# Delta-rule operands in DRAM: from one row per head to one region per fetch

## What is computed

```python
u    = tmat @ (v * beta);  wk = tmat @ (kb * exp(g))      # tmat: inverse of a unit triangular 64x64
attn = tril(q @ k.T * decay);  q_head = q * exp(g);  k_tail = k * exp(g_last - g)
def step(state, ...):                                     # one chunk after the other
    v_new = u_i - wk_i @ state
    o_i   = q_i @ state + attn_i @ v_new
    state = state * exp(gl_i) + k_i.T @ v_new
```

## Time and profile before

| | |
|---|---|
| median of 3 runs | 3933.44 us (3933.2 to 3941.19) |
| the profiled execution | 3942.79 us |
| its span | 3941.1 us |
| delta_prep | about 2660 to 2823 us of the span |
| rwkv_prep | to about 3207 us |
| scans | from 3207 us to about 3740 us |

### The profile page before, as it was taken

One profiled execution on the slowest core, in us unless ns is written; L12 is line 12 of the kernel. 1 busy time (PEld: TensorE's weight loads), 2 busy tenths in 40 slices (PEclk: granted clock), 3 DMA queues, 4 the chain that ended last, 5 costly groups with the idle time before them and its releaser, 6 DMA issues. The chain is left out here.

```text
span 3941.1 us, 64424 instructions
## 1 busy us (share of the span) xinstructions
PE 3479.2 (88%) x28352; PEld 2795.1 (71%) x28352; DVE 2077.9 (53%) x2261; ACT 665.9 (17%) x1080; POOL 786.8 (20%) x817
## 2 busy tenths in 40 slices
PE   6999999999998989889999999998677746588698
PEld 3777777777787878778888888886466535576586
DVE  2477777753333645545463353328687845233564
ACT  2122222212000001221111010002233301121100
POOL 0111111110000000025004306100276779100000
PEclk8999999999999999999999999998788867788899
DMA  9444444444332444322232223336767799676443
GB/s 401 147 150 150 151 154 148 150 175 158 124 119 109 162 175 162 118 86 83 84 111 89 86 95 119 112 125 215 232 176 189 193 237 193 161 204 206 141 170 107
DMA packets 359079, 607.74 MB, mean 154 GB/s; under 512 B 136440, under 2 KB 244080, under 8 KB 330128
## 3 DMA queue, kind: packets, MB, share of 16 engines
q1 hardware_dynamic: 305488, 472.23, 37.6%
q0 software_dynamic: 21712, 92.42, 7.2%
q10 hardware_dynamic: 31600, 38.99, 2.8%
HBM read 469.17 MB, written 134.39 MB: 153 GB/s over the span
## 5 line engine op out<-in xcount | busy, mean ns | idle before, releaser
L182 PE MATMUL front_ps<-b_hT,p_wb 128*128 128x512 f32 x4224 | 980.6, 392 | 6.8 <-PEq L94 6.8
L182 PEld LDWEIGHTS front_ps<-b_hT,p_wb 128*128 128x128 f32 x4224 | 790.7, 188 | 187.8 <-issue 20.6
L1772 PE MATMUL in_ps<-b_hT,in_wb 128*128 128x512 f32 (+1 forms) x3264 | 750.0, 390 | 13.5 <-DVE in_wb L1759 13.5
L1772 PEld LDWEIGHTS in_ps<-b_hT,in_wb 128*128 128x128 f32 (+1 forms) x3264 | 606.9, 187 | 147.8 <-DVE in_wb L1759 13.6
L1757 DVE CAST in_wb<-in_raw 128x2048 fp32r<-128x2048 f32 (+1 forms) x68 | 82.6, 1215 | 535.8 <-PE in_ps L1772 531.0
L170 DVE CAST p_wb<-p_raw 128x2048 fp32r<-128x2048 f32 x88 | 108.0, 1227 | 431.7 <-PE front_ps L182 420.8
L813 POOL DMA_DIRECT2D front_mwb<-in_w_ada x128 | 101.3, 796 | 795.8 <-PE front_mps L823 790.6
L1772 PEld LDWEIGHTS in_ps<-b_hc,in_wb 128*128 128x128 f32 (+1 forms) x1728 | 211.4, 189 | 3.2
L1772 PE MATMUL in_ps<-b_hc,in_wb 128*128 128x256 f32 (+1 forms) x1728 | 212.6, 283 | 0.0
L172 DVE TENSOR_TENSOR p_wb<-p_raw,p_wb 128x2048 fp32r<-128x2048 f32 x88 | 201.8, 2293 | 3.0
L1211 PE MATMUL mid_ps<-mid_wb,b_hT 128*128 128x512 f32 x768 | 179.5, 395 | 13.8 <-DVE mid_wb L1196 13.8
(11 more groups left out here) (457 smaller groups left out, 4314.4 us busy)
## 6 DMA issues: line engine op xcount, KB each, us to landing
p_raw<-in_w_in_tiles SPq DMA_DIRECT2D x88, 1024.0 KB, 6.0
in_raw<-in_w_in_tiles SPq DMA_DIRECT2D x67, 1024.0 KB, 4.8
front_mwb<-in_w_ada POOLq DMA_DIRECT2D x128, 512.0 KB, 5.0
open_wb<-in_w_ada_groups SPq DMA_DIRECT2D x32, 1024.0 KB, 11.3
g_scr<-gprep_ob SPq DMA_DIRECT2D x8, 3474.0 KB, 11.5
merge_raw<-in_w_branch_units SPq DMA_DIRECT2D x32, 512.0 KB, 4.5
mid_raw<-in_w_o_parts SPq DMA_DIRECT2D x32, 512.0 KB, 3.3
last_raw<-in_w_out_parts SPq DMA_DIRECT2D x32, 512.0 KB, 3.3
```

Source lines behind the costliest of these rows:

```text
L182: last = self.nc.tensor.matmul(self.ps[:, n % 2, :], self.wb[:, n % 2, x, kt, :], self.hT[:, y, kt, :], start=kt == term == 0, stop=kt == ...
L1772: last = self.nc.tensor.matmul(self.ps[0:width, n % 3, first:end], self.wb[:, n % 2, x, kt, 0:width], h[:, y, kt, :], start=kt == term == ...
```

## The change

The delta operands get two DRAM tensors in place of one. g_chan is indexed by chunk, direction, partition, head and column; g_tok by chunk, partition, head and column. So the heads of one partition lie side by side, and what one fetch takes from one partition is contiguous. The store becomes three DMAs per head, and self.stored counts 80 per head where it counted 48. The computation is untouched.

```diff
-            eng.wait_ge(self.stored[u], 48 * GH // 2)
+            eng.wait_ge(self.stored[u], 80 * GH // 2)
...
     def store(self, sp, i):
         u = i % 2
         sp.wait_ge(self.s["k_out"], i + 1)
-        sp.dma_start(self.g_scr[:, i:i + 1].rearrange("c h p x -> p (c h) x"), self.ob[:, u]).then_inc(self.stored[u], 16)
+        chan, tok = self.g_scr
+        for d in range(2):
+            sp.dma_start(chan[:, d, :, i:i + 1].rearrange("c p h x -> p (c h) x"),
+                         self.ob[:, u, :, G_CH * d:G_CH * (d + 1)]).then_inc(self.stored[u], 16)
+        sp.dma_start(tok[:, :, i:i + 1].rearrange("c p h x -> p (c h) x"), self.ob[:, u, :, 2 * G_CH:G_COLS]).then_inc(self.stored[u], 16)
...
             r = slice(64 * d, 64 * d + 64)
-            rows = self.g_scr[STEPS[k][d]].rearrange("h p x -> p h x")
-            sp.dma_start(self.chan[:, u, d], rows[:, :, G_CH * d:G_CH * (d + 1)]).then_inc(self.loaded[u], 16)
-            sp.dma_start(self.tok[r, u], rows[r, :, 2 * G_CH:G_COLS]).then_inc(self.loaded[u], 16)
+            chan, tok = self.g_scr
+            sp.dma_start(self.chan[:, u, d], chan[STEPS[k][d], d]).then_inc(self.loaded[u], 16)
+            sp.dma_start(self.tok[r, u], tok[STEPS[k][d], r]).then_inc(self.loaded[u], 16)
...
-    g_scr = dram("g_scr", (NCH, GH, P, G_COLS))
+    g_scr = (dram("g_chan", (NCH, 2, P, GH, G_CH)), dram("g_tok", (NCH, P, GH, G_TOK)))
```

More of the change, by code:

```diff
@@ L2485, in heads @@
         if i >= 2 and d == 0:
-            dve.wait_ge(self.stored[u], 48 * (i // 2))
+            dve.wait_ge(self.stored[u], 80 * (i // 2))
         dve.wait_ge(self.s["eg_out"], 2 * i + d + 1)
@@ L2525, in exponentials @@
         if i >= 2:
-            act_e.wait_ge(self.stored[u], 48 * (i // 2))
+            act_e.wait_ge(self.stored[u], 80 * (i // 2))
         self.alink(self.nc.scalar.activation(self.em[:, u], self.em[:, u], ACT.Exp))
```

## The result

The changed kernel takes 4009.34 us (median of 4 runs, 4000.93 to 4011.41) against 3936.21 us for the kernel before beside it (4 runs, 3933.2 to 3941.19): a ratio of 1.0172, with an interval of 1.0156 to 1.0188. That is 73 us slower, where I had forecast no change (3935 us, range 3926 to 3944). The profiled execution is one of 4000.93 us with a span of 3999.2 us, 58 us above that of before.

What follows compares the result with a forecast made beforehand. GpSimd's solver chain was taken to bound the scans, its start hanging on rwkv_prep and the end of delta_prep. Stores +2.7 us and fetches -1.0 us summed to +1.7 us, giving 3935 us on the median, range 3926 to 3944.

Steps and rivals of the forecast that it cites:

- The store, per head: delta_prep's store: 10.9 us against 9.05 per head, +1.8 us; bounds +1.2 and +4.8, priced from r_home's 528 B store.
- The loop over heads: delta_prep: products of head i wait for head i-2's store; 18.8 us of cover, so +1.8 fits without slowing the loop.
- the wait that I had named as a sign of error: delta_prep: VectorE waiting for a store inside the loop over heads would show the forecast wrong.
- The end of the stage, +2.7 us: delta_prep's end: last store issued 0.9 us late and 1.8 longer, +2.7 us; bounds +1.5 and +12.7.
- What it shifts: After delta_prep: the delay passes through rwkv_prep to GpSimd's batch and the end, with no slack seen; last write 2 to 4 us later.
- The fetch, -1 us: Scans, steps 9 to 11: channel part faster, 0.3 us a step; token part stays at 183 GB/s; -1 us in all.
- my other bound of -12.3: Scans' fetches: other bound of the three steps' gain, if the token part moved at 387 GB/s.
- The stores are slow: Rival, delta_prep: scattered 516 B writes at 216 GB/s; +12.7 - 1 = +11.7 us, 3945; chance 0.13.
- The token fetch speeds up: Rival, scans: small pieces were what slowed the token fetch; 2.7 - 12.3 = -9.6 us, 3924; chance 0.14.
- GpSimd isn't the bound: Rival, scans: TensorE's 34.4 us of token waits come off; 3901; chance 0.04.
- TensorE waits longer for its instructions: Rival, scans, steps 8 to 10: five stops in matmul runs grow 2 us each, +10 on +1.7, 3945; chance 0.09.
- The rule I had weighed: Stores: pieces from 512 B run at line rate, so store cost +0 and sum near -1 us; r_home's row spoke against it.

Runs made afterwards that it cites:

- e9: e6 with every piece written and fetched one column later, 4 B past a multiple of 64 B; 3978.85 us, ratio 1.0106 to the kernel before.
- e6: The changed kernel with DRAM rows padded to 144 and 336 columns, each piece beginning at a multiple of 64 B; 3944.20 us, ratio 1.0020.
- e8: The changed kernel with DRAM rows of 132 and 324 columns stored whole, both ends at multiples of 16 B; 3942.31 us, ratio 1.0016.
- e11: The changed kernel with full rows of 132 and 324 columns in DRAM and SBUF, one piece per partition and fetch; 3941.88 us, ratio 1.0011.
- e12: e9 with offset 7 columns instead of 1, so pieces begin 28 B past and end at a multiple of 32 B; 3944.32 us, ratio 1.0009.
- e13: The changed kernel with rows of 136 and 328 columns, pieces beginning at multiples of 32 B; 3940.03 us, ratio 1.0012.
- e16: The changed kernel with chunks' blocks moved apart by 16 unused rows each, partitions' distances unchanged; 3965.43 us, ratio 1.0088.
- e5: The kernel before with each head's store cut by chunks into three DMAs, pieces still 2316 B; 3935.56 us, ratio 0.9995.
- e14: The changed kernel, heads side by side, with partitions' blocks 4608 and 10752 B apart, which also moves chunks apart; 3964.94 us, ratio 1.0063.
- e10: Rows of 144 and 336 columns, heads 0 to 7 beginning 0, 16, 32, 4, 0, 8, 48, 12 B past a multiple of 64 B; 3967.63 us.
- e2: The kernel before, one array and one store per head, but heads side by side in DRAM, pieces 18528 B apart; 3939.48 us, ratio 1.0004.

## Why the prediction was wrong

**The store, per head.** This is the step that failed: the price of the store, "+1.8 us per head", with +4.8 as its upper bound. The runs show +9.3 us per head between the first store and the last, and the token store, the last of the three, lands after 22.1 us, where the single store landed after 11.5. I took r_home's 528 B store as the nearest row and called the two "strided in the same way". Their size was near; their ends weren't, nor was the distance between chunks (1,081,344 B there, 1,056,768 B in the change). A piece of 528 B beginning at a multiple of 528 has one end on a multiple of 32 B (528 is 16.5 times 32), and the pieces of 516 B in heads 1 to 6 have none. e9 against e6 shows what the ends cost, and e8, which has r_home's size, ends and distance, is quick. The upper bound was no bound either, because it was drawn from rows of that same store.

**The loop over heads.** I had found that it does not become slower. That was right for the cost I had put in, and e6, e8, e11 and e12, where the stores behave as priced, show no wait of VectorE for a stored buffer in the whole stage. With the real cost a head's stores outlast the 16.9 us that a head takes on VectorE, so the 18.8 us of cover are used up, and the wait that I had named as a sign of error is there with 53.3 us.

**The end of the stage, +2.7 us.** For small pieces as such, with one even end, the stage is 4.5 to 6.1 us longer (e6 to e8 and e11 to e13), and VectorE's idle time at its end grows by as much (21.32 us in e6, 15.77 before). This lies inside the recorded bounds of 1.5 and 12.7, but it is about twice the 2.7. The 516 B pieces of e6 move 276 GB/s where I had taken 302, and head 7's store is issued 2.4 us later than before, counted from head 0's, where I had 0.9. That rwkv_prep starts just 2.66 us late in e6 and e11 is luck: there the stage itself began earlier (2688.50 in e6, 2691.32 before). Of the change's 70.2 us the small pieces are 5.5 (e6), and what the forecast had no term for is the other 65: by e16 39 of them go with the distances between blocks and 26 with the crooked ends of six heads; in e9, with all eight heads crooked, the ends alone cost 37. No run has even ends in all heads at the slow distance, so the split between the two is that of this one path.

**What it shifts.** The stage's delay reached GpSimd's last write (71.4 us) with nothing absorbed, as the prediction had it. This step held.

**The fetch, -1 us.** The rates came as forecast: 389 for the channel part, 179 GB/s for the token part, in pieces of 10272 B. The packets say the same over several steps: one of 10272 B takes 0.75 us on average (3370 to 3495 us), eight of 1284 B took 0.85 before (3300 to 3420 us). So the size of the piece moves the token part's rate little. The Trainium skill (SBUF — State Buffer, on the DMA port swizzle) has 64 partitions at half the bandwidth, and the trace agrees: 179 beside 389 GB/s. In step 9 SP now reaches r_home 3.9 us after its first issue (7.9 before), but r_turn goes out at 3510.92, 71.1 us later than before, no sooner than the chain itself:

```profile
3495.70 0.33 SPq L3165 DMA_DIRECT2D all_gchan<-g_chan  x1
...
3499.64 2.17 SPq L3406 DMA_DIRECT2D scan_rops<-r_home  x1
...
3510.92 0.32 SPq L3409 DMA_DIRECT2D scan_rops<-r_turn  x1
```

The stretch from GpSimd's last write to the end was 13.3 us shorter, which looks like my other bound of -12.3. It is no gain of the fetch: e5, whose fetches are those of before, took 561.8 us there (3929.5 less 3367.75), the change 561.4, e11 565.2, and e14, with one-piece fetches, 573.6. That stretch varies by more than 10 us between executions, whatever the fetch.

**The rivals.** *The stores are slow* had the right place and side, but not the reason and too small a price. It blamed scattered writes of 516 B; those of e6 are scattered and quick (276 GB/s). It put 12.7 us on the stage, which lost 70.2, and said 3945, with a chance of 0.13. *The token fetch speeds up*: no (179 GB/s). *GpSimd isn't the bound*: no, the 8.6 us that the token waits lost went to scan_rinv. *TensorE waits longer for its instructions*: no. The stops of the earlier trace rows are now 3.64 and 4.21 us:

```profile
3506.19 1.64 PE L3466 MATMUL scan_rwork<-scan_ry,scan_rinv 64*64 64x64 f32 x44 [3.64 <-issue]
...
3513.78 0.43 PE L3459 MATMUL scan_gpx<-scan_rmid,scan_rinv 32*32 32x32 f32 x13 [4.21 <-issue]
```

**The rule I had weighed.** The Trainium skill (DMA: Bandwidth & Descriptors, Specifications) lets pieces from 512 B on run at line rate and has smaller ones read, modified and written back. Here pieces of 516 B ran at 145 to 163 GB/s with both ends crooked and at 276 with one even, so the size alone does not decide. The Trainium skill (Collectives: The Full Stack, Rules for kernel authors) asks for buffers at multiples of 32 B against such a read-modify-write; e10's two classes agree with that unit, though no row shows the mechanism. On distances, the Trainium skill (DMA: Bandwidth & Descriptors, Latency and other measured facts) reports copies slowed where the rows of neighbouring partitions lie a large power of two apart; a pad of 192 B did not help there, one of 4 KiB gave the full rate back. The slow distance here, 1,056,768 B between chunks, is 8192 B over 2 to the 20th; e8's, 32,768 B over it, was quick. So 8192 B over, twice the pad named there, do not help here, and whether the same thing is at work no run shows.

**What stays open.** Why one even end is enough; why pieces of 2316 B don't pay; which property of the distance does the harm. e16 moved the chunks of both arrays and the directions of the channel array at once, and with larger arrays also where the later ones begin in DRAM, so no run says which of these counts; the packets only show that pieces of both sizes were slow.

## What to carry to other kernels

Before stored pieces are made smaller or laid side by side, work out where both ends of each fall, modulo 32 B, over all heads and partitions: an odd row of 129 or 321 floats, packed without a gap, makes most pieces begin and end crookedly, and a pad to a multiple of 32 B took that cost away here (e13). Then try another distance between the blocks of one store before giving the layout up. A row of another transfer is a fair price only if it agrees in size, in ends and in distances. And a wait on the fetched operand (34.4 us here) is no prize while the next wait on the same engine is for another chain.

## What the runs showed of the hardware

- Stores of 516 B pieces, engines full: 268 to 279 GB/s with an end on a multiple of 32 B, 145 to 163 with neither (e10). Where the chunks lay 1,056,768 B apart: 180 with an even end, 115 with neither (heads 0 and 3 of the change). Pieces of 2316 B, six of eight with two crooked ends: 393 GB/s.
- A shift of all pieces by 4 B cost 37 us in eight heads (e9 against e6).
- 16 unused rows at the end of each block, with the pieces as crooked as before, gave 39 us back (e16 against the change).
- Small pieces as such, 4608 in place of 1536 a head with one end even, cost 4.5 to 6.1 us in eight heads (e6 to e8, e11 to e13).
- Three DMAs in place of one for the same pieces cost nothing (e5); neither did scattering pieces of 2316 B at 18528 B (e2).
- A fetch into 64 partitions moves 179 GB/s with pieces of 10272 B and 183 with pieces of 1284 B.
